# Hybrid decoder block on one core: expert weights laid out with 16 neighbouring rows per partition

## What is computed

```python
h = rmsnorm(x, g_pre_mix) * (1 + sc1) + sh1
y = hybrid_mixer(h, ...)                       # attention and a recurrence
x = x + gt1 * rmsnorm(y, g_post_mix)
h = rmsnorm(x, g_pre_ffn) * (1 + sc2) + sh2    # sc2, sh2: the second affine pair
# mixture of 32 experts (4 groups of 8), each token goes to 2 of them
lg = h @ w_group + b_group                     # (2048, 4)
le = h @ w_router + b_router                   # (2048, 32)
hid = silu(h @ w_gate[e]) * (h @ w_up[e])      # (2048, 512) each
y = y + (hid * cw[:, e]) @ w_down[e]           # (512, 2048)
x = x + gt2 * rmsnorm(y, g_post_ffn)
```

## Time and profile before

| | us |
|---|---|
| median of three runs | 1811.13 |
| the runs | 1808.51 to 1815.97 |
| span of the profiled execution | 1813.7 |
| TensorE busy | 1618.5 (89%) |
| VectorE busy | 551.6 (30%) |
| ScalarE busy | 214.2 (12%) |
| GpSimd busy | 14.2 (1%) |
| moved by DMA | 589.81 MB, 325 GB/s over the span |

### The profile page before, as it was taken

How to read it: one execution, slowest core, us unless ns; L and a number is a source line. 1 busy time by engine, 2 the same in 40 slices (tenths; PEclk the granted TensorE clock), 3 DMA queues, 4 the chain that set the end, 5 groups by cost and what they waited for, 6 DMA issues and landing times.

```text
span 1813.7 us, 20690 instructions
## 1 busy us (share of the span) xinstructions
PE 1618.5 (89%) x8413; PEld 892.6 (49%) x8413; DVE 551.6 (30%) x1145; ACT 214.2 (12%) x419; POOL 14.2 (1%) x19
## 2 busy tenths in 40 slices
PE   3679999999979999588999999999999999898995
PEld 1346776688856644344434444443444344344441
DVE  1335344274243300331323222232322222232223
ACT  1110000221201200300011101001110100011011
POOL 0000000000000010000000000000000000000000
PEclk9879999999988999889999999999999999999998
DMA  9998877425369955249999999999999999999993
GB/s 353 387 386 307 316 286 279 175 94 182 98 233 386 387 204 187 93 151 402 394 399 398 396 401 395 402 394 400 397 397 400 394 402 395 401 395 397 399 395 148
DMA packets 242164, 589.81 MB, mean 325 GB/s; under 512 B 6936, under 2 KB 7240, under 8 KB 224712
## 3 DMA queue, kind: packets, MB, share of 16 engines
q1 hardware_dynamic: 238176, 580.93, 85.3%
q0 software_dynamic: 992, 5.29, 0.9%
q10 hardware_dynamic: 2952, 2.95, 0.5%
HBM read 587.04 MB, written 2.11 MB: 325 GB/s over the span
## 4 chain that ended last, share of the span: by engine, by line
PE 50%; DMA 38%; SPq 7%; DVE 2%; issue 1%; ACT 1%; ACTq 0%; DVEq 0%
DMA ring<-in_w_up 34%; PE bank L815 14%; PE bank L492 14%; PE bank L477 12%; SPq L370 6%; DMA ring<-in_w_ada 4%; PE bank L432 2%; PE bank L447 1%; SPq L301 1%; PE bank L681 1%; PE bank L784 1%; PE bank L465 1%; PE bank L419 0%; PE bank L708 0%; PE bank L575 0%
## 5 line engine op out<-in xcount | busy, mean ns | idle before, releaser
L815 PE MATMUL bank<-ring,RN 128*64 128x512 f32 x2048 | 467.7, 609 | 58.6 <-DMA ring<-in_w_up 57.2
L815 PEld LDWEIGHTS bank<-ring,RN 128*64 128x64 f32 x2048 | 176.3, 140 | 343.0 <-issue 341.5
L842 PE MATMUL bank<-ring,RN 128*64 128x512 f32 x1024 | 226.8, 594 | 16.6 <-issue 16.6
L477 PE MATMUL bank<-RH,ring 128*128 128x256 f32 x1024 | 225.3, 380 | 0.0
L477 PEld LDWEIGHTS bank<-RH,ring 128*128 128x128 f32 x1024 | 193.3, 190 | 27.7 <-issue 1.9
L1628 DVE TENSOR_TENSOR RN<-bank,RN 64x512 f32<-64x512 f32 x32 | 22.2, 692 | 465.2 <-ACT RN L1093 465.2
L842 PEld LDWEIGHTS bank<-ring,RN 128*64 128x64 f32 x1024 | 84.6, 137 | 138.2 <-issue 138.2
L492 PE MATMUL bank<-ring,RH 128*128 128x512 f32 (+1 forms) x384 | 139.3, 521 | 0.0
L784 PEld LDWEIGHTS bank<-RN,RH 128*128 128x128 f32 x1024 | 118.4, 196 | 13.7 <-issue 12.2
L784 PE MATMUL bank<-RN,RH 128*128 128x128 f32 x1024 | 121.5, 281 | 1.4 <-DVE RN L1572 1.4
L801 PE MATMUL bank<-RG,RN 128*128 128x512 f32 x256 | 114.1, 599 | 1.6 <-DVE RG L1635 1.6
(11 more groups left out here) (276 smaller groups left out, 758.7 us busy)
## 6 DMA issues: line engine op xcount, KB each, us to landing
ring<-in_w_gate SPq DMA_DIRECT2D x64, 2048.0 KB, 17.6
ring<-in_w_up SPq DMA_DIRECT2D x64, 2048.0 KB, 20.6
ring<-in_w_down SPq DMA_DIRECT2D x64, 2048.0 KB, 17.7
ring<-in_w_ada SPq DMA_DIRECT2D x48, 2048.0 KB, 18.6
ring<-in_w_in SPq DMA_DIRECT2D x26, 2048.0 KB, 13.0
ring<-in_w_out SPq DMA_DIRECT2D x8, 2048.0 KB, 19.7
RX<-in_x ACTq DMA_DIRECT2D x2, 1024.0 KB, 10.3
RG<-gain_rows POOLq DMA_DIRECT2D x2, 1024.0 KB, 6.3
```

What stands on the lines that cost most here:

```text
L477: last = mm(bank[b][:, 0:S], ring[:, s0 + k // 8, k % 8, c:c + P], hT[:, k, :], start=k == 0, stop=k == KT - 1)
L815: last = mm(bank[0][64 * s:64 * s + 64, :], tokT[:, k, q * CAP:(q + 1) * CAP], ring[:, 2 * (k // 8) + s, k % 8, :], start=k == 0, stop=k = ...
L842: last = mm(bank[2 + n % 2][64 * (n // 2):64 * (n // 2) + 64, :], hidT[:, k * CAP:(k + 1) * CAP], wdn[:, n * BLK:(n + 1) * BLK], start=k = ...
```

## The change

The rows of the expert matrices are dealt out differently: row p * 16 + k of a matrix of 2048 rows goes to partition p, block k (row p * 4 + k for `w_down`). The 8 rows of a slot are then neighbours in HBM, one run of 16 KB for each partition, and so are the 2 rows of a slot of `w_down`. Three things follow that order. `xn2` is written with its features permuted, so that block b holds feature q * 16 + b at place q. The transposes of `hid` take every fourth column. The router's rows are read in the new order, and the second affine pair, which is formed in the old order, goes through HBM with the gains (`late_rows`, 64 rows in place of 32) and comes back permuted.

```diff
+KB = 16
+KA = KT // KB
-    gain_rows = nc.dram_tensor("gain_rows", [2 * KT, P], F32, kind="Internal").ap()
+    late_rows = nc.dram_tensor("late_rows", [4 * KT, P], F32, kind="Internal").ap()
-        gcol = RG[:, 1, 1888:1920]
+        lcol = RG[:, 1, 1888:1952]
+        gcol, acol = lcol[:, 0:2 * KT], lcol[:, 2 * KT:4 * KT]
+        def by_rows(w):
+            return w.rearrange("p (b q) -> p b q", b=KB)
+        def in_rows(w):
+            return w.rearrange("p (q b) -> p b q", b=KB)
-            wg = a["w_gate"].rearrange("e (k p) c -> e p k c", p=P)
-            wu = a["w_up"].rearrange("e (k p) c -> e p k c", p=P)
-            wd = a["w_down"].rearrange("e (k p) c -> e p k c", p=P)
+            wg = a["w_gate"].rearrange("e (p k) c -> e p (k c)", p=P)
+            wu = a["w_up"].rearrange("e (p k) c -> e p (k c)", p=P)
+            wd = a["w_down"].rearrange("e (p k) c -> e p (k c)", p=P)
             def expert_halves(e):
-                g, u, d = (w[bass.ds(e, 1)].rearrange("o p k c -> p (o k) c") for w in (wg, wu, wd))
-                return [g[:, 0:8, :], u[:, 0:8, :], g[:, 8:16, :], u[:, 8:16, :], d[:, 0:2, :], d[:, 2:4, :]]
+                g, u, d = (w[bass.ds(e, 1)].rearrange("o p x -> p (o x)") for w in (wg, wu, wd))
+                return [g[:, 0:4096], u[:, 0:4096], g[:, 4096:8192], u[:, 4096:8192], d[:, 0:4096], d[:, 4096:8192]]
             def dst_of(s):
-                return half(s) if s < 4 else ring[:, s, :, :].rearrange("p (k a) b -> p k (a b)", k=2)
+                return ring[:, s, :, :].rearrange("p a b -> p (a b)")
...
-                        inc(tr(bank[7][0:2 * KT, 0:P], gcol, ident), "gains_T")
+                        inc(tr(bank[7][0:4 * KT, 0:P], lcol, ident), "gains_T")
...
-                        last = tr(bank[1][:, f * P:(f + 1) * P], hid[:, f * P:(f + 1) * P], ident)
+                        last = tr(bank[1][:, f * P:(f + 1) * P], hid[:, f:4 * P:4], ident)
...
-            do(fn(xn2[:, 1, :], x_t[:, 1, :], ACT.Copy, scale=st[:, 5:6]), sig("xn2_ready_act"))
-            wait(act, "aff2_ready")
+            do(fn(by_rows(xn2[:, 1, :]), in_rows(x_t[:, 1, :]), ACT.Copy, scale=st[:, 5:6]), sig("xn2_ready_act"))
+            wait(act, "aff2_in", 32)
...
-            pool.dma_start(gain_rows, part[0:2 * KT, 0:P]).then_inc(sig("gains_out").sem, 16)
+            pool.dma_start(late_rows, part[0:4 * KT, 0:P]).then_inc(sig("gains_out").sem, 16)
...
+            for n in range(2):
+                src = late_rows[(2 + n) * KT:(3 + n) * KT, :].rearrange("k c -> (k c)").rearrange("(p b) -> p b", b=KB)
+                pool.dma_start(aff[:, 2 + n, :], src).then_inc(sig("aff2_in").sem, 16)
...
-            pool.dma_start(wrt[:, :, 0:NGRP], a["w_group"].rearrange("(k p) c -> p k c", p=P)).then_inc(sig("router_in").sem, 16)
-            pool.dma_start(wrt[:, :, NGRP:36], a["w_router"].rearrange("(k p) c -> p k c", p=P)).then_inc(sig("router_in").sem, 16)
+            pool.dma_start(wrt[:, :, 0:NGRP], a["w_group"].rearrange("(p k) c -> p k c", p=P)).then_inc(sig("router_in").sem, 16)
+            pool.dma_start(wrt[:, :, NGRP:36], a["w_router"].rearrange("(p k) c -> p k c", p=P)).then_inc(sig("router_in").sem, 16)
...
-            affine(1, vec[:, 1, V_GPRE2:V_GPRE2 + KT], 3 * KT, "aff2_ready")
+            affine(acol[:, 0:KT], acol[:, KT:2 * KT], vec[:, 1, V_GPRE2:V_GPRE2 + KT], 3 * KT, "aff2_ready")
...
-            step(v.tensor_copy(part[0:2 * KT, 0:P], bank[7][0:2 * KT, 0:P]), "gains_T_copied")
+            step(v.tensor_copy(part[0:4 * KT, 0:P], bank[7][0:4 * KT, 0:P]), "gains_T_copied")
...
-            do(ts(xn2[:, 0, :], x_t[:, 0, :], st[:, 4:5], None, ALU.mult), sig("xn2_ready"))
+            do(ts(by_rows(xn2[:, 0, :]), in_rows(x_t[:, 0, :]), st[:, 4:5], None, ALU.mult), sig("xn2_ready"))
+            wait(dve, "aff2_in", 32)
```

More of the change, by code:

```diff
@@ L871, in _ @@
                         for f in range(4):
-                            last = tr(bank[2][:, f * P:(f + 1) * P], dhid[:, f * P:(f + 1) * P], ident)
+                            last = tr(bank[2][:, f * P:(f + 1) * P], dhid[:, f:4 * P:4], ident)
                         last.then_inc(sig("dense_T").sem, 1)
@@ L1141, in _ @@
             for n in range(2):
-                src = gain_rows[n * KT:(n + 1) * KT, :].rearrange("(o k) p -> o (k p)", o=1).to_broadcast([P, D])
+                src = late_rows[n * KT:(n + 1) * KT, :].rearrange("(o k) p -> o (k p)", o=1).to_broadcast([P, D])
                 pool.dma_start(RG[:, n, :], src).then_inc(sig("gains_in").sem, 16)
+            for n in range(2):
+                src = late_rows[(2 + n) * KT:(3 + n) * KT, :].rearrange("k c -> (k c)").rearrange("(p b) -> p b", b=KB)
+                pool.dma_start(aff[:, 2 + n, :], src).then_inc(sig("aff2_in").sem, 16)
             for tt in range(TT):
                 pool.dma_start(x_t[:, tt, :], a["x"][tt * P:(tt + 1) * P, :]).then_inc(sig(f"x_again{tt}").sem, 16)
-            pool.dma_start(wrt[:, :, 0:NGRP], a["w_group"].rearrange("(k p) c -> p k c", p=P)).then_inc(sig("router_in").sem, 16)
-            pool.dma_start(wrt[:, :, NGRP:36], a["w_router"].rearrange("(k p) c -> p k c", p=P)).then_inc(sig("router_in").sem, 16)
+            pool.dma_start(wrt[:, :, 0:NGRP], a["w_group"].rearrange("(p k) c -> p k c", p=P)).then_inc(sig("router_in").sem, 16)
+            pool.dma_start(wrt[:, :, NGRP:36], a["w_router"].rearrange("(p k) c -> p k c", p=P)).then_inc(sig("router_in").sem, 16)
             wait(pool, "ring_used", USED["FULL"] + 2 * (OUT0 + 4))
@@ L1226, in _, with affine @@
                 ada_mod(n)
-            def affine(which, gpre, c_shift, ready):
+            def affine(scale, shift, gpre, c_shift, ready):
                 bada = vec[:, 0, V_BADA:V_BADA + 6 * KT]
-                scale, shift = aff[:, 2 * which, :], aff[:, 2 * which + 1, :]
                 do(tt_op(shift, mod[:, c_shift:c_shift + KT], bada[:, c_shift:c_shift + KT], ALU.add))
@@ L1236, in _ @@
             wait(dve, "mod_copied", ADA_DVE)
-            affine(0, vec[:, 0, V_GPRE1:V_GPRE1 + KT], 0, "aff1_ready")
+            affine(aff[:, 0, :], aff[:, 1, :], vec[:, 0, V_GPRE1:V_GPRE1 + KT], 0, "aff1_ready")
             def modulate(dst, which, ready):
```

## The result

The median went from 1812.29 us (four runs, 1808.51 to 1815.97) to 1739.98 us (four runs, 1738.80 to 1744.55). The ratio is 0.9603, with a 95% interval of 0.9584 to 0.9621: 72 us less. The forecast of 1752 us had the sign and the source of the gain, and was 12 us too high; its range (1741 to 1785 us) ended one microsecond above the measured median. The profiled span went from 1813.7 to 1737.0 us. A span lies 1.8 us under its execution's own time (1737.0 and 1738.80 here), so the span of before belongs to one of the slowest executions, near 1815.5 us, and the one of after to the fastest.

The account below looks back on a forecast made before the run. Loads bound the expert loop, TensorE close behind. Span 1813.7 + 1.5 (`xn2`) - 1.7 (TensorE's wait there) - 58.8 (30 periods, 31.66 to 29.7) = 1754.7 us, hence 1752 us; range 1741 to 1785 us.

Parts of the forecast that it names:

- the period in the sum: Loop over the experts: each expert's time falls from 31.66 to 29.7 us, saving 58.8 us over 30 experts.
- padding: Expert loop: loads and TensorE, within half a microsecond of each other, never interleave perfectly, so 29.7 us was taken per expert.
- What bounds the kernel: Expert loop: bound by its loads at 31.66 us an expert, with TensorE second at 29.3 us on average.
- The rate by packet size: Weight loads: 9 ns per packet plus 0.0370 ns per byte, so 16 KB takes 615 ns, 426 GB/s.
- TensorE's period: TensorE's work per expert: 29.3 us plus 0.3 for strided loads in the `hid` transposes, 29.6 us (29.3 to 29.9).
- the cross-check: Whole span: taking away all 57.2 us of TensorE's waits and adding 1.5 + 32 x 0.3 gives 1767.6 us.
- they go: Expert loop: TensorE's low-clock stretches vanish with the waits of 2 us, giving 1748 us; mostly expected.
- they stay: Expert loop: TensorE's low-clock stretches remain after the change, giving 1767.6 us.
- the text's own signs: What would show it: about 119000 packets, 418 to 428 GB/s throughout the loop, `w_up` waits under 20 us.
- The narrower forecast: Total time: 1740 to 1762 us, given a chance of 0.61.
- xn2: Permuted writes before the loop: +0.3 to +1.5 us once, 1.5 taken; VectorE 2.29 to 3.5, ScalarE 2.0 to 3.3 us.
- The affine pair through HBM: Two added GpSimd DMAs issue later loads 1.1 us later; cost nothing, under 70 us of cover.

## Why the prediction was right in its mechanism, and where it was wrong

The step that failed is the period in the sum: 30 periods of max(29.5 to 30.0, 29.3 to 29.9) us, taken at 29.7. Measured were 29.30 us. TensorE's term was off most, 29.6 us recorded and 29.12 measured, but with it put right the loads are the longer limit, so it counts only down to theirs. From 29.7 to 29.30 lead four steps: 0.1 us of padding; 0.1 because TensorE's 29.6 stood above the loads' 29.5; 0.14 because the loads ran at 428.5 and not 426 GB/s, 29.36 us; 0.06 for the head start with which TensorE enters the loop. Over 30 periods that is 12 us. The median was missed by 12 us, too: 9.7 in the loop, where something stands against the 12, and some 2 before it.

- *What bounds the kernel* was right: loads first, TensorE close behind. The edit that halves the loads shows TensorE's limit 0.2 us under the measured period, and the one that cuts the scatter shows the loads' pace unchanged.
- *The rate by packet size* was right and is the part that carried the gain: 426 GB/s forecast, 428.5 measured, and 4 and 8 KB on the same line. The 2.5 GB/s between them are 4 us over the loop. SP's issues fell to 0.33 us; from 4 KB on they were already near that while the rate still rose, so they didn't carry the gain there. Between 2 and 4 KB no run takes the two apart.
- *TensorE's period* was the term furthest off. Recorded were 29.3 us from the earlier trace rows, plus 0.3 for the transposes. Measured were 29.12 with the transposes, which cost 0.04. The 29.3 was read from the end of one wait to TensorE's next idle time, and so it holds the drain of the matmul pipeline: the down product of the changed kernel prints 7.09 us, but the next group starts 6.89 us after it (1064.28 to 1071.17). In the earlier trace rows these 0.2 us are part of the reading, because TensorE then waited. Without the wait the period is 29.3 - 0.2 = 29.1, as measured. The 0.3 came from VectorE's extra cost for each strided element, 0.6 ns, carried over to TensorE's 128 columns. The load did slow down by 64 ns (80 by that reckoning), but it runs mostly under the matmuls before it; the text had put it "straight on TensorE's path".
- *The padding* for two near-equal limits (29.7 in place of 29.6) was not needed: the two ran as max(29.12, 29.36) with a head start, 29.30 on average. Both terms together, 29.7 in place of 29.30, are 0.4 us a period, 11.6 us for 29 periods. Against it stands 1.6 us at the loop's head, where the down product of expert 0 ran at the lower clock for a part of its time (8.71 us, 7.09 before). So the loop gave 70.2 us where the text had 58.8 + 1.7 = 60.5, 9.7 of the 12 us by which the median was missed. The rest, some 2 us, lies before the loop.
- *The clock* was judged rightly in the cross-check: the low stretches inside the loop vanished with the waits of 2 us, and the span came out beyond the value for "they go" (1748), far from "they stay" (1767.6).
- *The range's lower end* was too high, by 1 us. The lowest case by the recorded bounds was 29.5 us a period and nothing for `xn2` but 0.3: 1813.7 + 0.3 - 1.7 - 30 x (31.66 - 29.5) = 1747.5 us of span, 1745 of median, and 1741 left 4 us below it. It didn't cover periods of 29.30 us (6 us less) and the 2 us before the loop. The 29.5 was the loads' bound, at the 426 GB/s of the line, although the text's own signs allowed 428; no faster loads stood in the sum. TensorE's bound of 29.3, the mean of two readings (29.07 and 29.56) that both hold the drain, was too high as well, so neither 29.36 nor 29.12 lay inside the bounds. The narrower forecast (1740 to 1762) began one microsecond below the range's own end, which is a slip of the text, and 1739.98 lies at its edge: how near the miss was is chance.
- *xn2* was priced at +1.5 us and cost 1.8, on ScalarE (3.77 us where 3.3 was the upper bound); VectorE's share was overpriced (1.96 us, 3.5 forecast, and under the 2.29 named as its least). *The affine pair through HBM* cost nothing, as said: no engine's list of waits has it, VectorE's wait for the gains stays at 13.9 us (13.8 before), and 70.3 of the 71.8 us of cover are left.
- *The median against the profiled span* was set at -2.6 us; the profiled execution of before had its span 2.6 us above the median that was known then, that of after has its span 3.0 us below its median. So the expected span was missed by 5.6 us more than the median.

## What to carry to other kernels

When a loop streams weights, compare the rate in stretches that carry different run lengths; two of them give a price per packet and per byte, and here the line through 2 and 8 KB foretold 4 and 16 KB within 1%. Lay weights out so that a partition's share of a transfer is one run, and put the permutation where it costs little: into a stationary operand whose loads are hidden, not into a ScalarE pass on the path. When the first limit is lifted up to the second, read the second between starts of groups that have no wait between them (a group's printed end holds a drain that is hidden when the next group follows at once), and let the case in which both come out well into the range.

## What the runs showed of the hardware

- A DMA engine's time for a packet from HBM to SBUF, worked out from the rates, was 85, 160, 311 and 612 ns for 2, 4, 8 and 16 KB: some 9 ns and the bytes at 27 GB/s. The distance made no difference where it was changed alone: 2 KB pieces lay 256 KB or 4 KB apart within a partition, both at 387 GB/s, and 16 KB runs began every 32 or every 16 KB, both at 428.
- A stationary operand read with a step of 16 bytes loaded in 205 ns in place of 141, and of the 64 ns four times an expert only 0.04 us reached the period. The Trainium skill (Advanced Engine Details and Errata, SBUF Cachelines) expects a penalty, without a size, where each access goes to another line of 16 bytes; the trace agrees for TensorE's loads, for ScalarE (2.00 to 3.77 us for 2048 elements at 64 bytes a step), and with a smaller penalty for VectorE (1.29 to 1.96 us).
- Writing with a step of 512 bytes in rows of 16 elements was slower than reading with a step of 64 bytes in rows of 128: 4.64 against 3.77 us on ScalarE, 2.88 against 1.96 us on VectorE.
